# A two-block transformer forward pass on one core: 13 of 16 pieces of x are turned by 32x32 blocks on VectorE and through DRAM instead of on TensorE

## What is computed

```
# first block, after three kinds of attention give y
x = x + y @ w_o
h = rmsnorm(x, ffn_norm);  x = x + (silu(dwconv(h @ w_gate)) * (h @ w_up)) @ w_down     # burst "ffn"
x = rmsnorm(x, final_norm)
# second block
c = rmsnorm(x, g_mix) @ w_in                                                            # burst "mix"
x = x + concat(mla(c), dsa(c)) @ w_out
q = rmsnorm(x, g_cross) @ w_q_cross;  x = x + cross_attention(q, mem) @ w_o_cross       # burst "cross"
x = x + square(relu(rmsnorm(x, g_mlp) @ w_up_2)) @ w_down_2                             # burst "mlp"
```

## Time and profile before

| | |
|---|---|
| median of 3 runs | 2344.11 us (2343.54 to 2344.15) |
| span of the profiled execution, first to last instruction | 2342.6 us |
| PE busy | 2329.2 us, 99% of the span |
| DVE busy | 1569.7 us, 67% |
| ACT busy | 1232.0 us, 53% |
| DMA queue of SP | 426.13 MB, its packets 55.3% of the 16 engines' time |
| granted TensorE clock, mean | 0.999 of full speed |

### The profile page before, as it was taken

How to read it: one execution, slowest core, us unless ns; L and a number is a source line. 1 busy time by engine, 2 the same in 40 slices (tenths; PEclk the granted TensorE clock), 3 DMA queues, 4 the chain that set the end, 5 groups by cost and what they waited for, 6 DMA issues and landing times.

```text
span 2342.6 us, 31399 instructions
## 1 busy us (share of the span) xinstructions
PE 2329.2 (99%) x12126; PEld 1990.3 (85%) x12126; DVE 1569.7 (67%) x2464; ACT 1232.0 (53%) x1877; POOL 4.3 (0%) x11
## 2 busy tenths in 40 slices
PE   9999999999999999999999999999999999999998
PEld 7888888888888888888888888888888888888887
DVE  7797877777777557755668556666766556556555
ACT  6566666555555445544656555656445345345343
POOL 0000000000000000000000000000000000000000
PEclk9999999999999999999999999999999999999999
DMA  8555455556555556565564545654555665655664
GB/s 313 171 162 179 137 168 165 178 183 204 182 180 206 191 178 204 181 219 189 165 205 156 177 152 161 226 181 159 192 188 181 206 189 180 204 192 182 216 194 153
DMA packets 119300, 436.20 MB, mean 186 GB/s; under 512 B 13392, under 2 KB 13648, under 8 KB 118128
## 3 DMA queue, kind: packets, MB, share of 16 engines
q1 hardware_dynamic: 117792, 426.13, 55.3%
q0 software_dynamic: 928, 7.47, 0.9%
q10 hardware_dynamic: 432, 0.60, 0.1%
HBM read 432.05 MB, written 2.10 MB: 185 GB/s over the span
## 4 chain that ended last, share of the span: by engine, by line
PE 98%; DVE 1%; DMA 1%; ACT 0%; issue 0%; SPq 0%
PE bank L511 30%; PE bank L493 16%; PE bank L495 16%; PE bank L494 16%; PE bank L525 16%; PE bank L575 1%; DMA x<-in_x 0%; PE bank L793 0%; PE bank L805 0%; PE bank L617 0%; PE bank L603 0%; PE bank L639 0%; DVE lo_w L1463 0%; PE bank L752 0%; PE bank L776 0%; PE bank L713 0%
## 5 line engine op out<-in xcount | busy, mean ns | idle before, releaser
L1463 DVE TENSOR_TENSOR lo_w<-raw_w,hi_w 128x1024 fp32r<-128x1024 f32 x804 | 965.0, 1218 | 537.9 <-ACT hi_w L994 536.6
L994 ACT ACTIVATE hi_w<-raw_w 128x1024 fp32r<-128x1024 f32 x804 | 833.9, 1053 | 581.8 <-PE bank L495 398.9
L511 PE MATMUL bank<-xT,hi_w 128*128 128x512 f32 x3008 | 720.9, 391 | 1.5 <-ACT hi_w L994 1.5
L511 PEld LDWEIGHTS bank<-xT,hi_w 128*128 128x128 f32 x3008 | 552.3, 188 | 108.4 <-DVE xT L1648 1.9
L525 PEld LDWEIGHTS bank<-xT,lo_w 128*128 128x128 f32 x3008 | 387.5, 191 | 17.2 <-DVE lo_w L1463 1.8
L525 PE MATMUL bank<-xT,lo_w 128*128 128x256 f32 x3008 | 396.4, 283 | 1.4 <-DVE lo_w L1463 1.4
L493 PE MATMUL bank<-hi_w,act_hi 128*128 128x512 f32 x864 | 336.4, 389 | 0.0
L495 PE MATMUL bank<-hi_w,act_lo 128*128 128x512 f32 x864 | 336.1, 389 | 0.0
L494 PE MATMUL bank<-lo_w,act_hi 128*128 128x512 f32 x864 | 336.1, 389 | 0.0
L493 PE MATMUL bank<-hi_w,xT 128*128 128x512 f32 (+1 forms) x672 | 265.4, 395 | 0.0
L495 PE MATMUL bank<-hi_w,xT 128*128 128x512 f32 (+1 forms) x672 | 260.9, 388 | 0.0
(11 more groups left out here) (339 smaller groups left out, 1565.3 us busy)
## 6 DMA issues: line engine op xcount, KB each, us to landing
raw_w<-in_w_up SPq DMA_DIRECT2D x216, 512.0 KB, 4.2
raw_w<-in_w_down SPq DMA_DIRECT2D x216, 512.0 KB, 3.5
raw_w<-in_w_gate SPq DMA_DIRECT2D x88, 512.0 KB, 4.2
raw_w<-in_w_in SPq DMA_DIRECT2D x72, 512.0 KB, 3.7
raw_w<-in_w_qk SPq DMA_DIRECT2D x64, 512.0 KB, 4.1
raw_w<-in_w_v SPq DMA_DIRECT2D x32, 512.0 KB, 3.6
raw_w<-in_w_o SPq DMA_DIRECT2D x32, 512.0 KB, 3.5
raw_w<-in_w_out SPq DMA_DIRECT2D x32, 512.0 KB, 3.6
```

The lines of the kernel that those rows point to most:

```text
L511: last = e.matmul(pair[c][:, :], hi_w[:, slot, at:at + P], both[:, kt].rearrange("p h t -> p (h t)"), start=(kt == 0), stop=(kt == g.kts - ...
L994: e.activation(hi_w[:, u % SPLIT_SLOTS, 0:unit_cols[u]], raw_w[:, u % RAW_SLOTS, 0:unit_cols[u]], ACT.Copy).then_inc(s["w_hi"], 1)
L1463: e.tensor_tensor(lo, raw_w[:, u % RAW_SLOTS, 0:unit_cols[u]], hi.bitcast(F32), ALU.subtract).then_inc(s["w_lo"], 1)
```

## The change

Thirteen pieces are no longer turned on PE: pieces 0 to 2 of ffn, mix and mlp, and all four of cross. Piece 3 of ffn, mix and mlp stays as it was. For a moved piece:

- DVE, right after the piece's addition, turns every 32x32 block of it into a new buffer `blocks` (`turn_blocks`, two instructions of 128 partitions x 512).
- SP writes `blocks` to a DRAM scratch (512 KB), waits for that to land, and reads it back into `gathered` (512 KB, in runs of 512 bytes, 1024 of them), which has two slots. These two DMAs stand in SP's list between the weight loads: loads go on up to unit last + 7, then SP waits for the blocks, writes, issues one load, waits for the write, reads back.
- ACT and DVE make the high and low parts from `gathered` (SBUF) instead of from PSUM (`gathered_hi`, `gathered_lo`), for ffn and mlp two, four or so units later in their lists than before.
- A partition then holds other channels of the piece than before, so the host lays the rows of w_in, w_gate, w_up, w_q_cross, w_up_2 and the gains in the same order (`by_partition`). The squares of o_late go to another junk buffer, since the new buffers lie where `y1` does.

The core of the diff (scratch, buffers and semaphores left out; the ACT side has the same places as the DVE side shown):

```diff
@@ straight_group, DVE
                     for t in range(TT):
                         add_straight(g, n, t)
+                    burst = {"o_late": "ffn", "down1_2": "mix", "out_late": "cross", "ox": "mlp"}.get(g.stage)
+                    if (burst, g.part) in MOVES:
+                        turn_blocks(burst, g.part)
+            def turn_blocks(burst, piece):
+                n = MOVES.index((burst, piece))
+                if n:
+                    e.wait_ge(s["blocks_out"], 16 * n)
+                for t in range(TT):
...
+                    e.transpose(blocks[:, t, :, :, :].rearrange("p b k j -> p k b j"),
+                                x[:, t, 512 * piece:512 * piece + 512].rearrange("p (k b f) -> p k b f", k=4, b=4)
+                                ).then_inc(s["blocks_turned"], 1)
+            def gathered_lo(burst, piece):
+                n = MOVES.index((burst, piece))
+                for k in range(4):
+                    kt = 4 * piece + k
+                    e.wait_ge(s["turned_hi"], 2 * TURNED0[burst] + kt + 1)
+                    e.scalar_tensor_tensor(by_blocks(xT[:, kt, 1, :]), gathered_tile(n, k), gain(burst, kt),
+                                           by_blocks(xT[:, kt, 0, :]).bitcast(F32), ALU.mult,
+                                           ALU.subtract).then_inc(s["turned_lo"], 1)
@@ sync_program
-            weights(8, n_units)
+            issued = 8
+            for n, (burst, piece) in enumerate(MOVES):
+                stage = {"ffn": "o_late", "mix": "down1_2", "cross": "out_late", "mlp": "ox"}[burst]
+                ahead = next(g.last for g in groups if (g.stage, g.part) == (stage, piece)) + 8
+                weights(issued, ahead)
+                e.wait_ge(s["blocks_turned"], TT * (n + 1))
+                e.dma_start(scratch[n].rearrange("t p r -> p t r"),
+                            blocks[:, :, :, :, :].rearrange("p t b k j -> p t (b k j)")).then_inc(s["blocks_out"], 16)
+                weights(ahead, ahead + 1)
+                e.wait_ge(s["blocks_out"], 16 * (n + 1))
+                if n >= 2:
+                    before, last = MOVES[n - 2]
+                    e.wait_ge(s["turned_lo"], 2 * (TURNED0[before] + 2 * last + 2))
+                e.dma_start(gathered[:, n % 2].rearrange("p t a k j -> p (t a) (k j)"),
+                            scratch[n].rearrange("t (a f) (b r) -> (f b) (t a) r", a=4, b=4)
+                            ).then_inc(s["blocks_back"], 16)
+                issued = ahead + 1
+            weights(issued, n_units)
@@ tensor_program, ffn (mlp the same; mix and cross likewise without their turns)
-            for piece in range(3):
-                units(1)
-                turn_x("ffn", piece)
-                units(1)
+            units(6)
```

More of the change, by code:

```diff
@@ L159 @@
 TURNED0 = {"y1": 0, "ffn": 8, "mix": 16, "ckv": 24, "cq": 25, "cross": 27, "mlp": 35}
+MOVED = {"ffn": (0, 1, 2), "mix": (0, 1, 2), "cross": (0, 1, 2, 3), "mlp": (0, 1, 2)}
+MOVES = [(burst, piece) for burst in MOVED for piece in MOVED[burst]]
+BLOCK = 32
+PE_TURNS = [("y1", pair) for pair in range(8)] + [("ffn", 6), ("ffn", 7), ("mix", 6), ("mix", 7), ("ckv", 0), ("cq", 0), ("cq", 1),
+                                                  ("mlp", 6), ("mlp", 7)]
 TILED0 = {"k_idx": 0, "k_r": 1, "q_idx": 2, "q_r": 6, "q_d": 8, "k_d": 12}
@@ L406, in junk_of @@
             if stage in ("attn", "o_late"):
-                return (v1 if stage == "attn" else y1)[:, t, part * 512:(part + 1) * 512]
+                return v1[:, t, part * 512:(part + 1) * 512]
             if stage == "out_late":
@@ L583, in turn_x @@
                 else:
-                    e.wait_ge(s["x_added"], add_count[{"ffn": "o_late", "cross": "out_late", "mlp": "ox"}[burst], piece])
+                    e.wait_ge(s["x_added"], add_count[{"ffn": "o_late", "mlp": "ox"}[burst], piece])
                 turn(burst, x, 2 * piece, 2)
@@ L891, in tensor_program @@
             e.wait_ge(s["row_copied"], 2)
[L892 to L895, removed]
+            units(18)
             units(2)
@@ L939, in tensor_program @@
             e.wait_ge(s["dsa_lo"], 8)
[L940 to L948, removed]
+            units(4 + 2 + 4 + 1 + 2 + 2)
             spread_row("mem", TURNED0["mlp"])
@@ L1321, in scalar_program @@
             e.wait_ge(s["w_used"], 2 * (last_unit["o_early"] + 1))
+            units(1)
             for piece in range(3):
[L1323 to L1328, removed]
+                units(2)
+                gathered_hi("ffn", piece)
+            units(1)
             e.wait_ge(s["w_used"], 2 * (last_unit["o_late"] + 1))
@@ L1335, in scalar_program @@
             e.wait_ge(s["w_used"], 2 * (last_unit["down1_1"] + 1))
+            units(3)
             for piece in range(3):
[L1337 to L1342, removed]
+                gathered_hi("mix", piece)
+                units(6 if piece < 2 else 5)
             turn_x("mix", 3)
@@ L1426, in scalar_program @@
             units(2)
+            units(1)
             for piece in range(3):
[L1428 to L1433, removed]
+                units(2)
+                gathered_hi("mlp", piece)
+            units(1)
             e.wait_ge(s["w_used"], 2 * (last_unit["ox"] + 1))
@@ L1989, in vector_program @@
             units(3)
+            units(1)
             for piece in range(3):
[L1991 to L1996, removed]
+                units(2)
+                gathered_lo("ffn", piece)
+            units(1)
             turn_x("ffn", 3)
@@ L2003, in vector_program @@
             units(6)
+            units(3)
             for piece in range(3):
[L2005 to L2010, removed]
+                gathered_lo("mix", piece)
+                units(6 if piece < 2 else 5)
             turn_x("mix", 3)
@@ L2083, in vector_program @@
             units(2)
-            turn_x("cross", 3)
+            gathered_lo("cross", 3)
             token_scales("cross", 8)
@@ L2098, in vector_program @@
             units(2)
+            units(1)
             for piece in range(3):
[L2100 to L2105, removed]
+                units(2)
+                gathered_lo("mlp", piece)
+            units(1)
             turn_x("mlp", 3)
```

59 lines of the change are left out of this document (43 added, 16 removed).

## The result

The changed kernel took **2354.65 us** (median of 4 runs, 2349.96 to 2356.96) against 2344.13 before: a ratio of 1.0042, 95% interval 1.0031 to 1.0054. It is slower by 10.5 us. The forecast was 2344.9, no change within 4.7 us, so that did not come; 2354.65 lies inside the range of 2337 to 2356, near its slow end.

A forecast was written before the change was run, and what follows sets the result against it. PE's list, busy 99% of the span, was taken to set the time. Turns -11.5, ffn and mlp 2 x 4.9, mix 0.3 and cross 2.2 summed to +0.8 us: 2344.11 becomes 2344.9, range 2337 to 2356.

The forecast's parts named there:

- Turns -11.5: PE's list: thirteen turns of x removed at 0.89 us each, 11.5 us gone.
- The road: A moved piece's way after its addition: block turn 1.3 us, write 3.4, read back 5.0, high and low parts 2.1.
- Rival A: Road as short as plain rows, read back 3.5 us: about -6 us, 2338; chance 0.15.
- Rival B: Slower road, X + Y of 9.5 us, or block turn twice the addition: +9.6 us, 2353.7; chance 0.28.
- X + Y: X is the write to DRAM, 3.4 us; Y the read back, 5.0; together 8.4, bounds 6.8 and about 11.
- The page's 3.2 us: A 512 KB DMA: about 2.0 us fixed plus bytes at 436 GB/s; would end the kernel some 9 us faster.
- ffn, 4.9 late: Burst ffn: piece 2's low parts at 423.3, PE wants them at 418.4; 4.9 us late, piece 1's 1.6 within it.
- mlp, 4.9: Burst mlp: same units apart and same pace as ffn, so another 4.9 us of waits.
- cross, 2.2: Burst cross: piece 3's low parts come 2.2 us late for PE's spread of the row of mem.
- mix, 0.3: Burst mix: pieces six units apart don't delay each other; 0.1 us for each of three pieces.
- SP's list at nothing: SP's waits with weight loads queued behind: about 5 us to spare in ffn, so costed at nothing.
- rival C: Forecast's waits, plus 1.8 us at half clock after two of them: +4.4 to +6 us, 2349.5; chance 0.09.

The follow-up runs named there:

- e1: Changed kernel without block turn, write and read back; high and low parts made straight from untransposed x (products of other numbers): 2339.56 us, ratio 0.9979.
- e10: e1 with piece 3's parts asked for one weight unit earlier on ACT and DVE in ffn and mlp: 2335.85 us, ratio 0.9966.
- e5: Changed kernel with blocks read back in runs of 2 KB instead of 512 bytes, in the wrong order: 2355.11 us, ratio 1.0048.
- e11: Changed kernel with write and read back issued by GpSimd on its own queue instead of by SP: 2373.42 us, ratio 1.0126.
- e6: Changed kernel with the parts of mix made two units later, after units 5, 11 and 17: 2350.7 us, ratio 1.0027.
- e2: Changed kernel with 14, 10 and 12 useless matmuls ahead of PE's long waits in ffn, cross and mlp: 2352.16 us, ratio 1.0035.
- e4_order: Changed kernel with the moved pieces' parts in ffn and mlp one unit later, after units 4, 6 and 8: 2352.12 us, ratio 1.0034.
- e7_seven: Changed kernel with only the seven pieces of mix and cross moved; ffn and mlp as in the kernel before: 2346.0 us, ratio 1.0010.
- e9: Changed kernel with only mix and cross pieces moved, mix's parts two units later, the spread of mem's row not held back: 2338.87 us, ratio 0.9980.

## Why the prediction was right and wrong, point by point

- **PE sets the time**: right. The kernel followed PE's waits and clock in every run.
- **Turns -11.5**: right. The lined-up starts give 11.6, in the changed kernel, e1 and e10 alike. The sign "PE's busy time down by some 11 us" did not come (3.1), since matmuls at the low clock and behind a restart count as busy.
- **The road**: right in its medians. Write 3.3 (3.4), read back 4.9 (5.0), block turn 1.29 us for two (1.3). Single roads took 7.6 to 10.1 us; where two overlapped, in ffn and mlp, writes took 5.0 to 5.9. Rival A had rested on Y = 3.5; e5 shows that even long runs take 4.5. Rival B's X + Y of 9.5 did not come either: its 2353.7 was nearly met, but by another mechanism, so that the time lies inside the range is in part luck. e11 has B's mechanism, and there it cost almost 30 us, low clock included, where B had 9.6.
- **The page's 3.2 us** for 512 KB, in the prediction by the Trainium skill (DMA: Bandwidth & Descriptors, "Anatomy of one DMA"): the write's 3.3 agrees, the read back's 4.9 does not. The page gives its formula for transfers issued by GpSimd; issued there, in e11, they took 3.4 and 5.8.
- **ffn, 4.9 late**: right, step by step. Piece 0's high parts ended at 408.0, as worked out; piece 2's block turn began at 411.42 (411.5), its data were back at 421.39 (421.2), its low parts complete at 423.6 (423.3). The waits were 1.4 + 3.6 = 5.0.
- **mlp, 4.9**: 4.5, and 0.6 for an addition that PE overtook, 5.1.
- **cross, 2.2**: 2.5.
- **mix, 0.3: wrong**, 3.4. The step that failed is "the pieces don't delay each other". ACT's wait of 5 us was seen. What follows on DVE was not: three low parts in a row and the next addition behind them, so that the writes of the second and third piece went out 17.9 and 18.4 us after the one ahead of each, where six units take 16.4. e6 shows it.
- **SP's list at nothing**: right. ACT's waits for loads of weights are 9.1 us in all, against 10.2 before.
- **What was missing from the sum**: the low clock, 5.8 us, which I had as rival C with 0.09, and the restarts and delays that no wait shows, 2.9 us. C's argument against itself, "the waits are short", was the mistake: the only row on it had a wait of 1.92 us, and waits of 3.3 and 2.2 us were in my own forecast. (For that row the half level is read from the starts, 0.43 us apart up to 5.5 us and 0.23 from there on; the profile has no clock record before 5.5 us.) e2 shows the effect apart from the wait.

Of the profile's +12.6, the forecast had +0.8. The waits that it mis-sized are 15.7 - 12.3 = 3.4, mostly mix; clock 5.8; restarts and delays 2.9. So most of the error is not in the road but in what a wait costs beyond its own length: the forecast put nothing there. By the prediction's own bar of 4.7 us this is the outcome "slower", which had 0.36, and not "same", which had 0.46.

The Trainium skill (TensorE: Matmul & The Clock Gate, Part 1) says that idle stretches bring the clock down. The trace agrees for the waits of 2.5, 3.0 and 3.6 us in the profiled run of the changed kernel; after 3.2 us in ffn of e4_order the clock stayed up.

## To carry to other kernels

Where one engine is the bound, an idle wait of 2 to 4 us in its list costs its length, a restart of some 0.3 us, and in many cases 1.5 to 2.6 us more in clock; put that into the sum, as a chance. Work moved off the bound engine pays only at places where its longer road is covered: price each place by itself, and move those alone (seven pieces gained 5 us, thirteen lost 10). Before taking work out, ask what stands in its shadow, since the next data may not come any sooner.

## What the hardware showed unexpectedly

- The granted clock after a wait isn't fixed. After 1.78 us it stayed up in ffn and fell in mlp, in one and the same run of e1_direct; in cross it was low after 2.32 us in e6_mixlater and stayed up after 2.33 in e7_seven. Of the 22 waits of 2.2 to 5.1 us within the traces of the changed kernel and its variants, 14 had the low clock behind them and 8 did not; the longest of these was 3.16 us (e4_order). What decides it is not shown. The runs of the kernels with long waits lie 2 to 7 us apart, those of e9, e10 and the kernel before 1 to 2.
- 512 KB read back from DRAM takes 4.9 us beside the weights in runs of 512 bytes, 4.5 in runs of 2 KB, and 5.8 on GpSimd's queue (medians of 13).
- DVE's 32x32 turn of 128x512 takes 0.69 us, 1.29 for two, about what an addition of that size takes (1.28 us for two).
